# One-hots of a retrieval layer: the gate multiply on GpSimd, five table rows per slab

## The reference, cut to what matters

```
q = tok @ w_q;  two top-16 searches over 128 sub-keys each; top 16 of their 256 sums
expert = i1 * 128 + i2;  gate = softmax(top_s)          # 8 heads x 16 = 128 experts per token
act = gelu(einsum('nd,nhkd->nhk', t, u_tab[expert]))
out = einsum('nhk,nhkd->nd', gate * act, v_tab[expert])  # u_tab, v_tab: 16384 x 1024 float32
```

## Time and profile before

| what | value |
|---|---|
| median of 3 runs | 2450.03 us (2446.65 to 2452.68) |
| the profiled execution's own time | 2446.26 us |
| its span (first to last instruction) | 2444.5 us |
| mean granted TensorE clock | 0.931 of full speed |
| PE / PEld busy | 2149.1 us (88%) / 1783.6 us (73%) |
| DVE busy | 1570.6 us (64%) |
| ACT / POOL busy | 748.1 us (31%) / 808.3 us (33%) |
| DMA | 682.81 MB, mean 279 GB/s |

### The profile page before, as it was taken

How to read it: one execution, slowest core, us unless ns; L and a number is a source line. 1 busy time by engine, 2 the same in 40 slices (tenths; PEclk the granted TensorE clock), 3 DMA queues, 4 the chain that set the end, 5 groups by cost and what they waited for, 6 DMA issues and landing times.

```text
span 2444.5 us, 34439 instructions
## 1 busy us (share of the span) xinstructions
PE 2149.1 (88%) x12253; PEld 1783.6 (73%) x12253; DVE 1570.6 (64%) x3259; ACT 748.1 (31%) x1111; POOL 808.3 (33%) x499
## 2 busy tenths in 40 slices
PE   7979999998769979999999888888889898998983
PEld 7978995554433439999999888888767676676662
DVE  1256215554452331199888677875888888989888
ACT  2122113443330012243444445443232323223221
POOL 2323320001110013366666511111634445565550
PEclk9989998999879989999999998998899899998996
DMA  9999987885995552155555666667999999999992
GB/s 349 347 350 350 346 305 316 320 316 199 320 338 187 181 199 87 51 166 169 174 169 169 209 244 228 236 230 261 359 394 394 393 393 376 393 394 394 394 371 100
DMA packets 200412, 682.81 MB, mean 279 GB/s; under 512 B 18432, under 2 KB 84352, under 8 KB 194304
## 3 DMA queue, kind: packets, MB, share of 16 engines
q1 hardware_dynamic: 151696, 508.36, 59.2%
q0 software_dynamic: 46080, 167.79, 18.1%
q10 hardware_dynamic: 2544, 5.48, 0.6%
HBM read 618.78 MB, written 196.32 MB: 333 GB/s over the span
## 4 chain that ended last, share of the span: by engine, by line
PE 34%; DMA 23%; issue 21%; DVE 14%; ACT 4%; POOL 3%; SPq 0%; ACTq 0%; DVEq 0%; POOLq 0%
DMA overlay<-peer_v 15%; PE bank L188 7%; PE bank L189 7%; PE bank L190 7%; DMA overlay<-peer_u 5%; DVE arena L1775 3%; DVE overlay L1952 3%; PE bank L1762 2%; POOL overlay L341 2%; PE bank L586 2%; PE bank L602 2%; DVE arena L1770 2%; POOL overlay L1401 2%; PE bank L625 1%; PE bank L652 1%
## 5 line engine op out<-in xcount | busy, mean ns | idle before, releaser
L188 PE MATMUL bank<-overlay 128*128 128x384 f32 (+4 forms) x2856 | 993.6, 348 | 145.2 <-DVE overlay L1956 88.4
L189 PE MATMUL bank<-overlay 128*128 128x384 f32 (+4 forms) x2856 | 973.0, 341 | 0.0
L190 PE MATMUL bank<-overlay 128*128 128x384 f32 (+4 forms) x2856 | 970.7, 340 | 0.0
L188 PEld LDWEIGHTS bank<-overlay 128*128 128x128 f32 x2856 | 561.2, 196 | 207.3 <-issue 112.3
L190 PEld LDWEIGHTS bank<-overlay 128*128 128x128 f32 x2856 | 558.7, 196 | 33.8
L189 PEld LDWEIGHTS bank<-overlay 128*128 128x128 f32 x2856 | 561.0, 196 | 30.5
L1401 POOL TENSOR_TENSOR overlay<-overlay 128x1024 fp32r<-128x1024 f32 x99 | 265.7, 2685 | 208.2 <-ACT overlay L1393 208.2
L1610 POOL DMA_INDIRECT arena<-peer_rows,arena x160 | 182.3, 1139 | 430.2 <-DVE arena L1770 410.3
L1610 POOL DMA_INDIRECT arena<-peer_v,arena x160 | 229.5, 1434 | 171.6 <-DVE arena L1775 158.8
L1775 DVE SCALAR_TENSOR_TENSOR arena<-arena 128x1024 f32<-128x1024 f32 x160 | 204.5, 1278 | 0.4
L1770 DVE SCALAR_TENSOR_TENSOR arena<-arena 128x1024 f32<-128x1024 f32 x160 | 193.7, 1218 | 7.2 <-DMA arena<-peer_rows,arena 7.2
(11 more groups left out here) (221 smaller groups left out, 2095.1 us busy)
## 6 DMA issues: line engine op xcount, KB each, us to landing
overlay<-peer_u SPq DMA_DIRECT2D x128, 512.0 KB, 3.7
overlay<-peer_v SPq DMA_DIRECT2D x128, 512.0 KB, 13.0
o_ks<-cache_k SPq DMA_DIRECT2D x16, 4088.0 KB, 27.4
o_vsall<-cache_vall SPq DMA_DIRECT2D x16, 4088.0 KB, 39.6
arena<-cache_kT SPq DMA_DIRECT2D x32, 896.0 KB, 11.2
arena<-cache_v SPq DMA_DIRECT2D x56, 512.0 KB, 6.8
arena<-w_out SPq DMA_DIRECT2D x48, 512.0 KB, 4.8
act<-arena SPq DMA_DIRECT2D x128, 192.0 KB, 1.9
```

What stands on the lines that cost most here:

```text
L188: pe.matmul(out, lhs[0], rhs[0], start=start, stop=False)
L189: pe.matmul(out, lhs[0], rhs[1], start=False, stop=False)
L190: return pe.matmul(out, lhs[1], rhs[0], start=False, stop=stop)
```

## The change

`hot_b` of a group is made by one DVE operation as `hot_a` is, 0 or 1 without the gate, and signalled on a new semaphore `hot_made`. POOL then multiplies the gates into it in place, one operation of 512 columns per group, and signals `hot_ready`, on which PE waits. ROW_TURNS has five places, (1, 2, 4, 5, 7), in place of three: 60 rows in the slab stage, 84 with the tail's 24 (before: 36 and 60), so 236 are left to the values stage in place of 260. POOL issues its gathers between the multiplies: one after each of the first slab's eight groups, then one after each group of ROW_TURNS.

```
-        ROW_TURNS = (2, 5, 7)
+        ROW_TURNS = (1, 2, 4, 5, 7)
...
-            for g in range(2 * UROWS):
+            pool.wait_ge(ch_kept, DT + 1)
+            for w in range(SLABS * GS):
+                pool.wait_ge(hot_made, w + 1)
+                pool.tensor_tensor(hot_b[:, w % 2], hot_b[:, w % 2],
+                                   slotT[:, 2, w * 4:w * 4 + 4].unsqueeze(2).to_broadcast([P, 4, P]), ALU.mult).then_inc(hot_ready, 1)
+                if w < RING:
+                    gather(w)
+                elif w % GS in ROW_TURNS:
+                    gather(RING + (w // GS - 1) * len(ROW_TURNS) + ROW_TURNS.index(w % GS))
+            for g in range(RING + (SLABS - 1) * len(ROW_TURNS), 2 * UROWS):
                 gather(g)
...
-                    for j in range(4):
-                        at = lambda row: slotT[:, row, w * 4 + j:w * 4 + j + 1]
-                        mm = dve.tensor_scalar(hot_b[:, w % 2, j], const("iota"), at(1), at(2), ALU.is_equal, ALU.mult)
-                    mm.then_inc(hot_ready, 1)
+                    dve.tensor_tensor(hot_b[:, w % 2], const("iota").unsqueeze(1).to_broadcast([P, 4, P]),
+                                      slotT[:, 1, w * 4:w * 4 + 4].unsqueeze(2).to_broadcast([P, 4, P]), ALU.is_equal).then_inc(hot_made, 1)
```

More of the change, by code:

```diff
@@ L1587, in layer @@
         u_lo2 = sem("u_lo2")
-        hot_ready, g_done, g_kept = (sem(n) for n in ("hot_ready", "g_done", "g_kept"))
+        hot_made, hot_ready, g_done, g_kept = (sem(n) for n in ("hot_made", "hot_ready", "g_done", "g_kept"))
         slab_stored = [sem(f"slab_stored{s}") for s in range(2)]
```

## The result

The changed kernel takes 2458.85 us, the kernel before 2446.65 us (medians of 19 runs each): a ratio of 1.0055, 95% interval 1.0042 to 1.0067, 12 to 13 us slower. The forecast was +17 us, slower, with a range of 2438 to 2488.

A forecast was written before the change was run, and what follows sets the result against it. The prediction took transfers to bound the values stage and a loop through several engines to pace the slab stage. Values stage -32, tail +5, slabs +33, first slab +11 gave +17, on 2450 a forecast of 2467 us, range 2438 to 2488.

The forecast's parts named there:

- The fourth rival: Values stage gives only half, -16 in place of -32, as PE keeps it: 2483 us; 0.16 together with rival 3.
- The slabs: Slab stage: each slab +3.0 us, between +2.3 and +3.2, for 11 slabs +33.
- The walk from `low` to group 5: Slab stage, loop behind the late fetch: group 5 ends 9.0 to 9.9 us after `low` starts, before 6.69.
- The port sum: Slab stage: DVE and POOL operations taking turns, 3.39 us a group, 27.1 us a slab against 25.3.
- both bounds: Slab stage: port sum (+1.8 us a slab) and loop behind the late fetch (+2.3 to +3.2) bite in turn: +3.0.
- the exclusion: Slab stage: of a DVE two-input operation and POOL's multiply, whichever comes second waits until the first is done.
- rival 2: Slab stage: no exclusion for comparisons and dots; slabs +8 for 11, total -11, 2439 us; chance 0.14.
- DVE's own saving: Slab stage: new `hot_b` saves 3.4 us a slab, two more dots cost 2.3; DVE gains 1.1 us.
- The first slab: Start of slab stage: multiply waits for POOL's entry, dots for gathers at 7.4 us: +11, between +5 and +13.
- The tail: Tail: five more gathers issued at its start, beside the `peer_u` fetch: +5, between 0 and +7.
- Rival 1: Slab stage: multiplies fall mostly into idle time, a slab costs +1; total -5, 2445 us; chance 0.18.
- Rival 3: Slab stage: gathers land after more than 12 us and DVE waits, +2 us a slab: 2489; 0.16 with the fourth rival.

The follow-up runs named there:

- e2: The kernel before with five dots per slab at (1, 2, 4, 5, 7), one-hots staying on DVE: 2434.72 us, ratio 0.9964 to the kernel before.
- e1: The changed kernel with three dots per slab at (2, 5, 7), multiply still on POOL: 2469.32 us, ratio 1.0108 to the kernel before.
- e3: The changed kernel with POOL writing `hot_b` by four memsets instead of the multiply, gates left out: 2429.62 us, ratio 0.9944 to the kernel before.
- e4: The changed kernel with gathers issued one slab earlier, so the ring stays 8 ahead: 2450.26 us, ratio 1.0032 to the kernel before.
- e5: The kernel before with five dots per slab at (0, 1, 2, 5, 7), one-hots on DVE: 2426.27 us, ratio 0.9927 to the kernel before.
- e6: The changed kernel with its five dots at (0, 1, 2, 5, 7): 2476.94 us, ratio 1.0146 to the kernel before.
- e7: The kernel before with six dots per slab at (0, 1, 2, 2, 5, 7), gelu earlier: 2414.67 us, ratio 0.9885 to the kernel before.
- e8: The kernel before with eight dots per slab at (0, 1, 1, 2, 2, 5, 7, 7), gelu earlier: 2388.94 us, ratio 0.9772 to the kernel before.

## Why the prediction was right

**What bounds the kernel.** Right for the values stage: 34 us for 24 rows (12.6 MB at 382 GB/s are 33), in every run with 84 rows the same 613 to 616 us, 600 with 96 and 567 with 120. The fourth rival (half of it) is out.

**The slabs.** +3.0 predicted, +3.1 measured. The walk from `low` to group 5 held: its 9.0 and 9.9 us stand against 8.9 in six of ten slabs and 9.8 in four, and 2.7 of the 3.1 us lie behind the start of `low`, the other 0.4 before it. But two pieces of the reasoning behind the number are to be corrected. The port sum of 3.39 us per group is too long: DVE's `hot_a` starts 3.19 us apart in the timeline above (1510.83 to the next pair's at 1514.02), because a multiply of 1.04 us holds DVE up only some 0.84 (1.52 - 0.68). With that the sum is 8 x (1.20 + 0.84) + 3 x 1.14 + 5 x 1.15 = 25.5 us, hardly above the 25.3 of before; so it is hardly this bound that makes the slabs long, but the loop. That +3.0 leaned on both bounds in turn and still came out is in part luck. And the loop is lengthened by both parts of the change: the rows alone give +2.0 (e2), the multiply alone +2.3 (e1), both together +3.1, less than their sum. The start of group 5 isn't what falls short: it comes 2.0 us later in e1, 1.15 in e2 and 3.2 in the changed kernel, which is their sum. What follows doesn't add: group 5 goes at its slow pace in all ten slabs of e1 and of e2, but in four of the changed kernel's. I had costed the dot behind pair 4 only together with the multiply, and written that all 33 us rest on the exclusion, although rival 2 kept 8 of them without it; e3 gives the exclusion at most 2.0 us a slab, 22 of the 33.6.

**The exclusion.** Shown by e3 with the durations beside it. The rule of the Trainium skill, "SBUF — State Buffer", section "Who interferes with whom", agrees in both halves here: the comparisons and POOL's reading multiply hold each other up (medians of 1.51 us for `hot_a` and 1.77 us for the multiply), behind the start of a dot the multiply took 1.95 us, and beside a POOL operation that only writes no `hot_a` is held up (0.684 us, at most 0.694). It says the loser waits for the whole instruction; DVE's loss was 0.84 us beside a multiply of 1.04 us. Times on POOL are rough in this profile, so the 0.2 us between them don't settle whether the hold is shorter; 0.84 is the number that the sums above need.

**DVE's own saving.** The sum said 1.1 us a slab less work. It is there: in e3 DVE is busy 190.0 us over the ten slabs, with 50 dots, against 199.7 before, with 30. In the changed kernel it is given back as waiting inside `hot_a`, which counts as busy: 240.5 us over the same ten slabs.

**The first slab** was mis-sized: +4 in place of +11. First multiply, first gather, first dot:

```profile
1381.85 1.04 POOL L1615 TENSOR_TENSOR arena<-arena 128x512 f32<-128x512 f32 x1 [7.54 <-DMA arena<-arena]
1383.06 1.13 POOL L1610 DMA_INDIRECT arena<-peer_rows,arena  x1 [0.17 <-issue]
```
```profile
1387.55 1.23 DVE L1779 SCALAR_TENSOR_TENSOR arena<-arena 128x1024 f32<-128x1024 f32 x1 [7.26 <-DMA arena<-peer_rows,arena]
```

The structure is as walked (POOL's entry wait holds the first multiply; DVE stands 7.3 us at the first dot), but the row came 4.5 us behind its issue. I took the 7.4 us of the earlier trace rows, where eight gathers had been issued in a row; here they come one at a time. The minimum of the earlier trace rows, 4.3 us, was the better row.

**The tail** was mis-sized the other way: +10 in place of +5, beyond my end of +7. The mechanism is confirmed by e4. The first fetch lost the 6.2 us of the extra bytes, for which I had worked out up to 6.7 us and then taken 5; e4 gives back 6.8 of the 10.1 us. The other 3.3 aren't explained; e3 and the changed kernel have long tails (73.7, 75.1), e2, whose gathers aren't tied to the multiplies, has 62.5.

**The sum.** The first slab came out 7 us below its term and the tail 5 us above; the two nearly cancel, so a total only some 3 us off (+13.7 by stages against +17) is in part luck. The sign isn't: the slabs' +33.6 against the values stage's -34 cancel, so the two small terms decide it, and both were forecast with the right sign.

**The rivals.** Rival 1 (the slabs absorb it) is out: +3.1 and not +1. Rival 2 (no exclusion) is out by e3. Rival 3 (short lead) didn't come in the changed kernel: DVE waited 7.9 us in all for gathered rows, nearly all at the first dot. A relative of it that I hadn't named is real: rows at other places make the late fetch slower (e5, e6, e7, e8).

## What to carry to other kernels

Where a stage's pace is set by a loop through several engines, moving work to an idle engine helps only if it leaves the loop's path shorter; find the operation that stands between the late arrival and the consumer, and keep new work out of exactly that place. VectorE and GpSimd were not two free engines here: a GpSimd multiply that takes 1.04 us alone cost the VectorE operation behind it 0.84 us, and VectorE was busy 0.63 us longer per group on average than in e3 (240.5 against 190.0 us over 80 groups), more than the 0.43 us that the change had taken off it. So count such a multiply on VectorE's time as well. And try the payload of a change (here the moved rows) without the part that is meant to make room for it: here it fitted by itself.

## What the runs showed that I had not expected

- The late fetch, 512 KB behind a 2 MB store, depends on where the gathers fall: 9.1 us before, 10.5 with the dots before the late `low` (e5, e7), 11.9 with eight dots (e8).
- PE's granted clock falls behind some of its waits. In the slab of the changed kernel shown above PE was idle 2.45 and 1.57 us before groups 4 and 5; the granted clock was 0.50, the lower of its two levels (1.2 of 2.4 GHz), from 1515.0 to 1519.2 and 1.00 again from 1519.5. Group 5 took 2.08 us at that clock, where it takes 1.16 at the full one, and the next matmuls of e2 stood in the chain at 0.32 us each, later ones at 0.17 to 0.18. The kernel before has it too (0.50 from 1472.1 to 1478.0), and by its 2.08 us group 5 ran so in all ten slabs of e1 and e2, in four of ten of the changed kernel although PE waits in each; what decides it isn't shown. The granted clock was 0.87 over the ten slabs of e2 and 0.91 before.
- A slab stage with DVE busy 93% (e8: 310 of 332 us) was only 1.5 us per slab slower than one with 78%.
